# Reordering the first layers' work: keys ahead of the Fourier products, convolution in steps of two taps, modulation products spread, turns posted sooner

## The reference, cut to what matters

```python
mx = split(silu(c) @ w_ada[l] + b_ada[l], 6); mc = the same of c_ctx      # shift, scale, gate, twice
hx = modulate(rmsnorm(x, g_pre_mix[l]), mx[0], mx[1])                    # also for the 256 context tokens
z = hx @ w_in[l]                       # q, k, v, output gate, 16 gate columns, fourier, conv (a, gate)
q, k = dwconv(z[q, k], w_qk_conv)      # 3 taps
h = mlstm_chunked(q, k, v, gates)      # 4 heads, forwards and backwards, 6 chunks of 128 in this kernel
yf = real part of a DFT over tokens and channels of z[fourier]
yv = silu(layernorm(dwconv(a * sigmoid(gate), w_dw, 31 taps)))
x = x + mx[2] * rmsnorm(concat(h, yf, yv) @ w_out[l])
x = x + mx[5] * rmsnorm(square(relu(modulate(rmsnorm(x), mx[3], mx[4]) @ w_mlp1)) @ w_mlp2)
```

## Time and profile before

| | before |
|---|---|
| median of 3 runs | 3354.8 us |
| profiled execution: its time / its span | 3353.06 us / 3351.3 us |
| mean granted TensorE clock | 0.942 |
| PE busy / PEld busy | 3051.1 us (91%) / 2452.1 us (73%) |
| DVE / ACT / POOL busy | 1417.9 / 1009.1 / 1046.3 us |
| first layer 0 up to its output product | 0 to 488.8 us of the span |
| first layer 1 up to its output product | about 1177 to 1528 us |

### The profile page before, as it was taken

How to read it: one execution, slowest core, us unless ns; L and a number is a source line. 1 busy time by engine, 2 the same in 40 slices (tenths; PEclk the granted TensorE clock), 3 DMA queues, 4 the chain that set the end, 5 groups by cost and what they waited for, 6 DMA issues and landing times.

```text
span 3351.3 us, 41178 instructions
## 1 busy us (share of the span) xinstructions
PE 3051.1 (91%) x16748; PEld 2452.1 (73%) x16748; DVE 1417.9 (42%) x2601; ACT 1009.1 (30%) x1640; POOL 1046.3 (31%) x508
## 2 busy tenths in 40 slices
PE   6899779899999979967999998999889989998898
PEld 4688568788888857756777776777667767776676
DVE  4584442513324256243521134644472246534822
ACT  3213432312213231333332232233423322334232
POOL 1121114222222412214244442232245423332455
PEclk9999878999999889978899989999999889999999
DMA  5332341111111123321222222122112222121121
GB/s 201 120 113 106 114 164 58 57 63 64 63 63 63 53 82 113 120 95 63 92 94 95 92 67 80 60 69 65 60 56 78 77 70 70 63 64 63 57 70 69
DMA packets 77708, 275.39 MB, mean 82 GB/s; under 512 B 8512, under 2 KB 10304, under 8 KB 77392
## 3 DMA queue, kind: packets, MB, share of 16 engines
q1 hardware_dynamic: 75824, 268.91, 23.8%
q10 hardware_dynamic: 1696, 3.84, 0.3%
HBM read 270.62 MB, written 2.10 MB: 81 GB/s over the span
## 4 chain that ended last, share of the span: by engine, by line
PE 78%; DVE 12%; ACT 4%; issue 3%; POOL 2%; DMA 1%; SPq 0%; DVEq 0%; ACTq 0%; POOLq 0%
PE pb L1011 19%; PE pb L1013 18%; PE pb L1012 18%; PE pb L1121 2%; PE pb L1033 2%; PE pb L1035 2%; PE pb L1034 2%; PE pb L960 2%; POOL RGR L2575 1%; PE pb L1051 1%; PE pb L1052 1%; PE pb L1053 1%; PE pb L1079 1%; DMA RG<-in_W_dram 1%; DVE AR L2071 1%
## 5 line engine op out<-in xcount | busy, mean ns | idle before, releaser
L2575 POOL TENSOR_TENSOR RGR<-RG,WHI 128x1024 fp32r<-128x1024 f32 x354 | 864.4, 2442 | 1861.0 <-ACT WHI L2164 1860.7
L2164 ACT ACTIVATE WHI<-RG 128x1024 fp32r<-128x1024 f32 x354 | 370.5, 1047 | 387.0 <-PE pb L1013 288.3
L1011 PE MATMUL pb<-HI,WHI 128*128 128x512 f32 (+1 forms) x880 | 376.9, 428 | 25.1 <-POOL RGR L2575 7.8
L1013 PE MATMUL pb<-LO,WHI 128*128 128x512 f32 (+1 forms) x880 | 354.5, 403 | 0.0
L1012 PE MATMUL pb<-HI,RGR 128*128 128x512 f32 (+1 forms) x880 | 354.4, 403 | 0.0
L1011 PE MATMUL pb<-HR,WHI 128*128 128x512 f32 (+1 forms) x768 | 278.9, 363 | 16.8 <-POOL RGR L2575 10.1
L1013 PE MATMUL pb<-HR,WHI 128*128 128x512 f32 (+1 forms) x768 | 277.7, 362 | 0.0
L1012 PE MATMUL pb<-HR,RGR 128*128 128x512 f32 (+1 forms) x768 | 277.5, 361 | 0.0
L1013 PE MATMUL pb<-HIDR,WHI 128*128 128x512 f32 (+1 forms) x768 | 274.8, 358 | 0.0
L1011 PE MATMUL pb<-HIDR,WHI 128*128 128x512 f32 (+1 forms) x768 | 273.8, 356 | 1.1 <-ACT RLT L2310 0.8
L1012 PE MATMUL pb<-HIDR,RGR 128*128 128x512 f32 (+1 forms) x768 | 274.2, 357 | 0.0
(11 more groups left out here) (407 smaller groups left out, 5622.3 us busy)
## 6 DMA issues: line engine op xcount, KB each, us to landing
RG<-in_W_dram SPq DMA_DIRECT2D x504, 512.0 KB, 3.5
XCX<-in_xT_dram ACTq DMA_DIRECT2D x4, 512.0 KB, 12.2
out_dram<-XCX SPq DMA_DIRECT2D x8, 256.0 KB, 2.1
CS<-in_CST_dram ACTq DMA_DIRECT2D x1, 1027.0 KB, 4.9
XCC<-in_ctxT_dram SPq DMA_DIRECT2D x4, 256.0 KB, 13.9
CS<-in_CST_dram SPq DMA_DIRECT2D x1, 523.0 KB, 4.8
RG<-in_W_dram SPq DMA_DIRECT2D x2, 256.0 KB, 2.9
RG<-in_W_dram SPq DMA_DIRECT2D x2, 128.0 KB, 3.4
```

What stands on the lines that cost most here:

```text
L1011: e.matmul(out, hi[:, k, :], xh, start=k == order[0], stop=False)
L1013: i = e.matmul(out, hi[:, k, :], xl, start=False, stop=k == order[7])
L2164: e.activation(WHI[:, u % 2, 0:n], RG[:, s % RING, 0:n], ACT.Copy).then_inc(*up("weightsA", u))
L2575: e.tensor_tensor(RGR[:, s % RING, 0:n], RG[:, s % RING, 0:n], WHI[:, u % 2, 0:n].bitcast(F32), SUB).then_inc(*up("weightsG", u))
```

## The change

A `run` posts all but the last of `after` behind each part. `rest` spreads the queued adas evenly over its steps, at least 1.5 steps apart, where it put one after every second step. The keys' first two slabs are laid before the slabs of the second DFT, no ada is taken in that DFT, and the fill's credit is set to -17 before the keys; the keys no longer wait in `end(prep)`, which comes after them. The convolution's steps have two taps at half the period. In first layer 1 the fill's period is 24 and not 10. More mLSTM steps are woven between `lnA` and `lnB` and behind them. At the start, ada (0, 10) comes before the first reciprocal root and not after it, and `place` doesn't put a split among the `modSplit` steps.

```diff
--- before.py
+++ after.py
@@ -201,6 +201,8 @@
         for part in parts:
             self.step("mm", n, part)
             self.early()
+            while len(self.after) > 1:
+                self.step("post", self.after.pop(0))
             self.weave(us / len(parts))
         for m in self.after:
             self.step("post", m)
@@ -259,9 +261,12 @@
     def rest(self, side):
 
         self.beside.remove(side)
+        every = max(1.5, len(side["steps"]) / max(1, len(self.fills)))
+        due = every
         for i, what in enumerate(side["steps"]):
             self.step(*what)
-            if i % 2 and self.fills:
+            if i + 1 >= due and self.fills:
+                due += every
                 before, self.soon = self.soon, []
                 self.ada(*self.fills.pop(0))
                 for m in before:
@@ -335,11 +340,13 @@
             self.run(p, [(0, 1)], gn / 512 * 3.4)
         self.after.append(p)
 
-    def products(self, jobs, banks=(0, 1), together=0):
+    def products(self, jobs, banks=(0, 1), together=0, abreast=True):
         tasks = jobs if together else self.tasks(jobs)
         made = 0
         for i, task in enumerate(tasks):
-            if i < together:
+            if i < together and not abreast:
+                made = max(made, together)
+            elif i < together:
                 made = together
                 if i == together - 1:
                     self.abreast(tasks[0:together], banks)
@@ -410,7 +417,8 @@
             if unit["slab"] >= RING:
                 free = taken[self.slabs[unit["slab"] - RING]["last"]]
                 at = max(at, free)
-                while at + 1 < first[u] and begin[at + 1] < begin[free + 1] + 5.5 and begin[at + 1] < begin[first[u]] - 3.6:
+                while at + 1 < first[u] and begin[at + 1] < begin[free + 1] + 5.5 and begin[at + 1] < begin[first[u]] - 3.6 and self.steps[
+                        at + 1][0] != "modSplit":
                     at += 1
             while self.steps[at][0] == "mm" and self.pieces[self.steps[at][1]]["kind"] == "ada" or self.steps[at + 1][0] == "mm" and self.pieces[
                     self.steps[at + 1][1]]["kind"] == "ada" and begin[at + 1] < begin[first[u]] - 5.0:
@@ -530,14 +538,14 @@
     if l == 0:
         o.fill(8.5, (0, range(16, 48, 2), "w_ada", 0), (1, range(0, 40, 2), "w_ada", 1))
     else:
-        o.fill(10.0, (2, range(0, 24, 2), "ada_w_2", 0), (3, range(8, 20, 2), "ada_w_2", 1))
+        o.fill(24.0, (2, range(0, 24, 2), "ada_w_2", 0), (3, range(8, 20, 2), "ada_w_2", 1))
     o.products(cu, (0, 1, 6, 7), 2)
     o.gates(l, tag, (0, 1, 6, 7))
     prep = o.begin([("mPrep", l, i) for i in range(5)], 5.0, -6.0)
     o.products([F(2576, 256, "glu", "evacA", go)], (0, 1, 6, 7))
-    conv = o.begin([("conv", l, j, t0, tn, k0) for j in range(2) for t0, tn, _ in oregs for k0 in range(0, 31, 4)], 3.6 if l == 0 else 5.0)
+    conv = o.begin([("conv", l, j, t0, tn, k0) for j in range(2) for t0, tn, _ in oregs for k0 in range(0, 31, 2)], 1.8 if l == 0 else 2.5)
     o.products([F(2064, 256, "u", None, go)], (0, 1, 6, 7))
-    o.end(prep)
+    keys = None
     for t0, tn, _ in oregs:
         n = tn // 128
         for ti in range(n):
@@ -546,6 +554,9 @@
                 p = o.piece("dftA", [], [o.bank((0, 1, 6, 7))], [by], l=l, j=j, ti=ti, t0=t0, how="ab")
                 o.last["ab", l, t0, by] = p
                 o.run(p, [ALL8], 0.5)
+        if t0 == NC:
+            keys = o.ahead([F(512, 512, "qk", "evacV", GB, dst="K")])
+            o.credit = -1.0e6
         b = [o.bank((0, 1, 6, 7)), o.bank((0, 1, 6, 7))]
         if n == 2:
             s = [o.slab("dft256", 0, 2 * h, 2, 0, 256) for h in range(2)]
@@ -554,15 +565,19 @@
         p = o.piece("dftB", s, b, ["evacV", "evacA"], l=l, t0=t0, tn=tn, nt=n, how="four")
         o.last["four", l, t0] = p
         o.run(p, [(i, j) for i in range(len(s)) for j in range(2)], n * 4 * 0.86 * tn / 512)
-    o.products([F(512, 512, "qk", "evacV", GB, dst="K"), T(1024, 512, "v", None, at=[[2, 3, 4], [5, 2, 3]]), F(0, 512, "qk", "evacV", go, dst="Q")],
-               (0, 1, 6, 7))
+    o.credit = -17.0
+    o.products(keys, (0, 1, 6, 7), 2, False)
+    o.end(prep)
+    o.products([T(1024, 512, "v", None, at=[[2, 3, 4], [5, 2, 3]]), F(0, 512, "qk", "evacV", go, dst="Q")], (0, 1, 6, 7))
     o.end(conv)
     o.period = 4.0
     stages = o.begin(mlstm_stages(l), 1.5)
     o.products([F(1536, 512, "og", "evacA", go)])
     for t0, tn, _ in oregs:
         o.run(o.piece("lnA", [], [o.bank()], ["evacV"], l=l, t0=t0, tn=tn, how="lnA"), [ALL8], 1.7)
+        o.weave(3.0)
         o.run(o.piece("lnB", [], [o.bank()], ["evacA"], l=l, t0=t0, tn=tn, how="lnB"), [ALL8], 1.7)
+    o.weave(4.5)
     for j in range(4, 8):
         o.step("mxSplit", l, j)
     o.rest(stages)
@@ -658,9 +673,9 @@
         o.step("xsum", 2 * pair + 1)
         o.adas(0, (2 * pair,), "w_ada", 0)
     o.step("xsums")
-    o.adas(0, (8,), "w_ada", 0)
+    o.adas(0, (8, 10), "w_ada", 0)
     o.step("rstd", "x0a")
-    o.adas(0, (10, 12, 14), "w_ada", 0)
+    o.adas(0, (12, 14), "w_ada", 0)
     o.flush()
     for l in range(2):
         first_layer(o, l)
@@ -1663,7 +1678,7 @@
             a = MX[:, 6 + j, t0:t0 + tn]
             if k0 == 0:
                 e.wait_ge(*at("evacV", ("glu", o.last["glu", l, "evacA", None])))
-            for k in range(k0, min(31, k0 + 4)):
+            for k in range(k0, min(31, k0 + 2)):
                 f = off31[t0] - 15 + k
                 u, wk = CU[:, j, f:f + tn], VC[:, wd + 2 * k:wd + 2 * k + 1]
                 if k == 0:
```

## The result

The changed kernel takes 3319.96 us (median of 4 runs, 3314.17 to 3321.84), the one before 3354.91 in the same session; the ratio is 0.9893, 95% interval [0.9876, 0.9911]. The profiled execution took 3320.43 us with a span of 3318.4 us, so 32.6 and 32.9 less than before. The forecast was 46 less, and 3309 as a median.

What follows compares the result with a forecast made beforehand. PE, with 78% of the chain, was taken to set the time, so gains come only where it waits or runs slowly. Nine parts sum to -46 us; 3353.1-46+1.7 gives 3309 us, range 3288 to 3342.

Steps and rivals of the forecast that it cites:

- The sign: Whole kernel: faster than before, below 3344.7 us, chance 0.87.
- Parts 1 and 5: Keys in first layers 0 and 1: slabs laid ahead end PE's wait for weights and its low clock; -10, -9 us.
- Part 2: Inside layer 0's keys: one ada left of three, the 5.03 us wait for DVE goes; -6 us.
- Part 3: Layer 0's last steps: mLSTM steps fill waits, more adas stand in a row; net -1 us.
- Parts 4 and 6: Layer 1: gates' preparation wait mostly returns, -1 us; fill period 24 takes five adas from products, -7, free in last steps.
- Part 7: Layer 1's last steps: mLSTM steps fill the 4.87 us wait before `lnB`, PE work keeps the clock up; -4 us.
- Part 8: Turns in both second layers: DIQ turns posted earlier shorten PE's 3.27 us wait for an ada's add; -7 us.
- Part 9: Start: split ahead of `modSplit`, an extra ada before the root; -1 us. Two taps a step cost nothing.
- B: Rival: DVE becomes the bound of the keys; 3326 us, chance 0.20.
- C: Rival: the keys' weights are still late, parts 1 and 5 bring nothing; 3328 us, chance 0.09.
- D: Rival: adas are not free in the last steps of both first layers; 3328 us, chance 0.13.
- E: Rival: slower, the adas' own ping-pong stops the mLSTM chain in the last steps; 3367 us, chance 0.08.

Runs made afterwards that it cites:

- e5: Changed kernel with the keys' first two slabs laid behind those of the second DFT again, in both first layers; 3322.25 us, ratio 0.9893.
- e10: Kernel before with only no ada from the second DFT product on and the credit at -17 ahead of the keys; 3348.35 us, ratio 0.9978.
- e8: e7 with the credit ahead of layer 0's keys at -34 and the fill's last eight adas moved behind the output product; 3303.01 us, ratio 0.9841.
- e9: e7 with the credit ahead of layer 0's keys at -34, all the fill's adas left in the last steps; 3300.14 us, ratio 0.9833.
- e3: Changed kernel with the spacing of before in `rest`, one ada behind every second step; 3316.98 us, ratio 0.9883.
- e2: Changed kernel without the two added weaves (between `lnA` and `lnB`, and behind them); 3311.54 us, ratio 0.9866.
- e7: Changed kernel with the added weaves in layer 1 alone and the gates' preparation steps 3 and 4 later in layer 1; 3307.13 us, ratio 0.9848.
- e11: Kernel before with only the fill's period of layer 1 at 24 and not 10; 3336.89 us, ratio 0.9946.
- e6: Changed kernel with the fill's period in layer 1 at 10 and not 24; 3337.03 us, ratio 0.9937.
- e1: Kernel before with only the lines in `run` that post all but the last of `after` behind each part; 3343.39 us, ratio 0.9959.
- e4: Changed kernel with the start of before: ada (0, 10) after the first reciprocal root, splits allowed among the `modSplit` steps; 3318.17 us, ratio 0.9881.

## Why the prediction was right, and where not

The sign, the chance of 0.87 and the range held (3320 in 3288 to 3342). The sum was 13 us too good, and that it was no more is in part luck: terms that were too good by 17 us in all, and 7 us in stretches for which it had no term (+2.3, +1.0, +1.2, +2.3, +0.4, none beyond the spread), stand against 11 us by which others were too cautious (parts 4 to 6 together, and 8).

*Parts 1 and 5 (-10 and -9; measured -7.9 and -5.6).* The view was right, the cause half wrong. "The DFT's four slabs and an ada's two hold the ring" was the cause; "laid ahead" was not the cure. With the ada gone the ring holds four and two, and the splits are ready whichever is laid first (e5, e10). A test would have been to count the ring without the ada. In layer 1, 2.7 of the gain is missing because `dftB` now starts behind the wait of 6.72, at low clock.

*Part 2 (-6; -4.6).* The reason "without adas DVE may lag" was right (e8 and e9, with no ada there, never wait), but one ada was left, behind the fourth key's first piece, and it met the old wait (5.28 us). I counted it and charged it 1.4. e9 shows what it cost: 8.4 us with its clock.

*Part 3 (-1; +6.0), the step that failed.* Forecast: waits -7, adas in a row +6. PE's idle time did fall by 7.4. Two adas more cost 7 by themselves (e10: 131.0 to 138.0). What the sum lacked is that PE's work in the filled stretch ran slower: 84.6 us at the lower clock for 68.9, and half of the 15.7 more is 7.8 (an estimate that takes PE as busy in it). That is more than half of the 13.4 us by which its busy time grew. Weaves and spacing are each worth 6 to 11 us against e10's 138.0 (e3: 129.7; e2 and e7: 126.9 and 131.7), but together only 1 to 4 (134.3 to 137.0 in four kernels). Why they cancel isn't settled, and e10 differs from those kernels in more than weaves and spacing (the convolution's steps, the place of `end(prep)`), neither of which was run alone; the times follow the low clock (59.5 us in e3, 53.8 and 68.9 in e2 and e7, 74.9 in e10, 84.6 in the changed kernel).

*Parts 4 and 6 (-1 and -7; together with keys to output gate -14.9).* That ACT's evacuation would stand behind step 3 came as foretold, 6.72 us. "5 x 1.4" was mis-sized: e11's four adas took 16.9 us with them, 8.3 of it ahead of the keys (part 5) and 8.6 for the other three, and e6's four cost 16.7. In the keys and values of e6 the price was near the forecast (1.7); the rest came as PE's wait for DVE at `dftA` and as low clock behind a wait that was there anyway, and why the one more ada lets the first come wasn't followed. "So 0" for their price in layer 1's last steps was right within 4 us (102.8 us with 5, 104.1 with 7, 103.1 to 107.2 in the kernels with 11, 105.2 with 14).

*Part 7 (-4; +1.4).* The wait of 4.87 before `lnB` fell to 1.82, but the chain of the mLSTM lost nothing: it now waits 8.81 us at one place. In layer 0 and layer 1 I took a wait of PE for a loss of the chain. "More PE work keeps the clock up" didn't come either: in layer 1 PE's busy time grew from 64.0 to 76.0 us and the clock stayed at 0.77, in layer 0 it grew and the clock fell.

*Part 8 (-7; -14.5, e1: -12.7).* The right steps, half the size in these executions. I costed one wait and one low stretch. The wait was sized right: PE is idle 3.1 us less in each second layer. DVE's last turn instruction, 2.72 us beside a split before, takes 0.69 at its earlier place. Around the turns two of three low stretches went; but e10, with the turns as before, has one there as well, so how many come is in part chance, and against e10's 603.8 the gain is 1.4 to 4.7 us a layer. The rows of DVE in the changed kernel:

```profile
2009.12 0.69 DVE L1548 TENSOR_TENSOR AR<-AR 128x512 f32<-128x512 f32 x1
2012.22 0.16 DVE L1529 TENSOR_TENSOR MOD<-pb,VC 128x2 f32<-128x2 f32 x1 [2.41 <-PE pb L1157]
```

*Part 9 (-1; +0.1, and e4 shows no difference).* Right within what can be told. The 2.3 us up to the second `dftB` are within the spread: e3 to e6 have 83.0 to 86.1 us there (before 82.3, changed 84.6). That two taps a step cost nothing was not run by itself.

*The rivals.* B: in layer 0's keys of the changed kernel DVE was busy 35.61 of 42.60 us (third of the busy times in the row) and made PE wait once, so it was half there.

```profile
149.00:191.60 42.60, 37.32 (x215) 31.21 (x214) 35.61 (x51) 7.93 (x12) 7.17 (x3) 0.96 0.24 87
```

C fell in both layers. D was right for layer 0 and wrong for layer 1. E fell: no chain of adas stopped the mLSTM.

## What to carry to other kernels

Before a transfer is moved, count who holds its buffers: removing one small holder did here what the reordering was written for. In a stretch where a chain over several engines sets the pace, judge a filling by the end of the chain and by the granted clock, not by PE's idle time. Side work with waits of its own belongs where the engine is idle anyway; in a full stretch it cost 1.0 to 8.3 us apiece (e6, e8, e11) instead of 1.4. And where short waits are many, the same steps came out 4 to 5 us apart in one stretch here, mostly by the clock: read a gain of that size from several executions, or from a row.

## What the hardware showed that I had not expected

- A tiny DVE instruction pays for a large POOL one: 128x8 took 2.28 us instead of 0.17 beside a split, and a serial chain of such instructions passed 4.2 us on to PE.
- The same list of steps took 126.9 and 131.7 us in two executions, with 53.8 and 68.9 us at the lower clock. Behind the same wait of 2.17 us the clock stayed at 1.00 in the changed kernel and fell to 0.50 for 10.2 us in e6.
- PE can be nearly always busy and stay at the lower clock: from the adas at the end of layer 0 to the output product's first matmuls, in the changed kernel, it was busy 23.4 of 26.0 us, all of it at 0.50 (1.2 GHz); ahead of that it had been idle for 2.32 us, until DVE's add of the ada before:

```profile
463.00:489.00 26.00, 23.35 (x147) 14.63 (x148) 7.97 (x31) 5.75 (x11) 7.22 (x4) 0.50 0.72 260
```
